# Two model blocks in one kernel: the second block's projection chunks over four PSUM banks, four small transfers on another queue, the last branch's gated product left in its bank

## The reference

```python
# first block
h = rms_norm(x, mix_norm_g)
ys, gate_logit = _token_mixers(h, w_in, ...)       # four kinds of attention, 4 heads of 64 each
branch = einsum('bsnc,ncd->bsnd', ys, w_branch)    # four branches, 256 -> 1024
gates = sigmoid(gate_logit)
x = x + sum(gates * branch, axis=2) @ w_out
x = x + square(relu(rms_norm(x, mlp_norm_g) @ w_up)) @ w_down
x = rms_norm(x, final_norm_g)
# second block
proj = rms_norm_2(x, norm1_g) @ w_in_2             # 1024 -> 2560: q, k, v (512 each), u (1024)
q, k = apply_rope(rms_norm_2(q, ...)), apply_rope(rms_norm_2(k, ...))
attn = moba_attention(q, k, v)                     # 8 heads of 64; with 256 tokens causal softmax attention
conv = conformer_conv(u, ...)                      # GLU, causal depthwise conv of 31 taps, layer norm, silu
x = x + concatenate([attn, conv]) @ w_out_2
x = x + (silu(h @ w_gate_2) * (h @ w_up_2)) @ w_down_2
```

## Time and profile before

| | |
|---|---|
| median of 3 runs | 812.22 us (812.01 to 813.08) |
| the profiled execution's own time | 809.01 us |
| its span | 807.2 us |
| PE busy | 782.7 us, 97% of the span |
| DVE busy | 477.3 us, 59% |
| ACT busy | 408.3 us, 51% |
| POOL busy | 44.2 us, 5% |
| transfers | 136.25 MB, mean 169 GB/s |
| granted TensorE clock | 1.0 in all 40 slices |

### The profile page before, as it was taken

One profiled execution on the slowest core, in us unless ns is written; L12 is line 12 of the kernel. 1 busy time (PEld: TensorE's weight loads), 2 busy tenths in 40 slices (PEclk: granted clock), 3 DMA queues, 4 the chain that ended last, 5 costly groups with the idle time before them and its releaser, 6 DMA issues.

```text
span 807.2 us, 9725 instructions
## 1 busy us (share of the span) xinstructions
PE 782.7 (97%) x3930; PEld 657.4 (81%) x3930; DVE 477.3 (59%) x623; ACT 408.3 (51%) x542; POOL 44.2 (5%) x38
## 2 busy tenths in 40 slices
PE   7999999999999999999999999989999999999998
PEld 5887889878888878888888887767987888888896
DVE  6654364656766877554445448589956654545434
ACT  6565455455656636455444446555556443443341
POOL 1000000000001410000000005011000000000000
PEclk9999999999999999999999999999999999999999
DMA  9842424434445356555655555736123654655341
GB/s 331 319 158 84 151 79 158 149 112 158 156 158 189 124 193 226 198 184 175 208 176 188 180 186 186 283 111 207 56 60 134 224 195 172 207 165 200 104 157 53
DMA packets 68509, 136.25 MB, mean 169 GB/s; under 512 B 2417, under 2 KB 7153, under 8 KB 67825
## 3 DMA queue, kind: packets, MB, share of 16 engines
q1 hardware_dynamic: 68000, 134.44, 49.0%
q10 hardware_dynamic: 464, 1.20, 0.4%
HBM read 134.43 MB, written 1.05 MB: 168 GB/s over the span
## 4 chain that ended last, share of the span: by engine, by line
PE 85%; DVE 9%; ACT 2%; issue 2%; POOL 1%; DMA 1%; SPq 0%; ACTq 0%; DVEq 0%; POOLq 0%
PE b L579 19%; PE b L581 19%; PE b L580 18%; PE SS L579 4%; PE SS L581 4%; PE SS L580 4%; PE TT L548 4%; PE OO L579 2%; PE OO L581 2%; PE OO L580 2%; DVE wlo L1502 2%; DVE ca L1972 1%; PE OO L893 1%; PE SS L662 1%; PE b L719 1%
## 5 line engine op out<-in xcount | busy, mean ns | idle before, releaser
L1502 DVE TENSOR_TENSOR wlo<-raw,whi 128x2048 fp32r<-128x2048 f32 (+2 forms) x123 | 274.2, 2230 | 160.8 <-ACT whi L1061 160.5
L1061 ACT CAST whi<-raw 128x2048 fp32r<-128x2048 f32 (+2 forms) x123 | 227.9, 1854 | 127.5 <-PE b L581 88.0
L579 PE MATMUL b<-whi,Ahi 128*128 128x512 f32 (+2 forms) x568 | 222.2, 391 | 7.4 <-ACT ust L1337 3.4
L581 PE MATMUL b<-whi,Alo 128*128 128x512 f32 (+2 forms) x568 | 215.3, 379 | 0.0
L580 PE MATMUL b<-wlo,Ahi 128*128 128x512 f32 (+2 forms) x568 | 214.7, 378 | 0.0
L579 PEld LDWEIGHTS b<-whi,Ahi 128*128 128x128 f32 x568 | 107.2, 189 | 28.2 <-ACT ust L1337 3.8
L581 PEld LDWEIGHTS b<-whi,Alo 128*128 128x128 f32 x568 | 107.0, 188 | 20.7
L580 PEld LDWEIGHTS b<-wlo,Ahi 128*128 128x128 f32 x568 | 107.4, 189 | 18.3
L579 PE MATMUL b<-whi,Bhi 128*128 128x512 f32 x154 | 60.9, 395 | 0.0
L581 PE MATMUL b<-whi,Blo 128*128 128x512 f32 x154 | 60.0, 390 | 0.0
L580 PE MATMUL b<-wlo,Bhi 128*128 128x512 f32 x154 | 60.0, 390 | 0.0
(11 more groups left out here) (273 smaller groups left out, 1027.0 us busy)
## 6 DMA issues: line engine op xcount, KB each, us to landing
raw<-in_w_in SPq DMA_DIRECT2D x40, 1024.0 KB, 4.9
raw<-in_w_up SPq DMA_DIRECT2D x16, 1024.0 KB, 5.4
raw<-in_w_dn SPq DMA_DIRECT2D x16, 1024.0 KB, 5.0
raw<-in_w_d SPq DMA_DIRECT2D x11, 1024.0 KB, 4.9
raw<-in_w_g SPq DMA_DIRECT2D x10, 1024.0 KB, 4.9
raw<-in_w_u SPq DMA_DIRECT2D x10, 1024.0 KB, 5.0
raw<-in_w_out SPq DMA_DIRECT2D x8, 1024.0 KB, 4.9
raw<-in_w_br SPq DMA_DIRECT2D x4, 1024.0 KB, 4.9
```

Of the source, the lines that this page charges most:

```text
L579: e.matmul(dst, xh, H[:, kc, c0:ce], start=first and kc == krs[0], stop=False)
L581: ins = e.matmul(dst, xl, H[:, kc, c0:ce], start=False, stop=last and kc == krs[-1])
L1061: e.copy(whi[:, s, 0:m], raw[:, r, 0:m]).then_inc(s_hi, 1)
L1502: e.tensor_tensor(wlo[:, s, 0:m], raw[:, r, 0:m], whi[:, s, 0:m].bitcast(F32), ALU.subtract).then_inc(s_lo, 1)
```

## The change

The second block's chunks go to banks (1, 2) and (0, 7) by turns (`P2B`). The four transfers from `odd` to `hp` are issued by SP, between the first two loads of the second block's output weights, and `phases` is gone from ACT; the two constants are copied at step 1 instead of step 9. `rturn` uses banks 5 and 6 by turns. DVE takes the row sums `r0` ahead of the weight split that is due at the same step. One of the 62 taps moves from step 14 to the end of the head loop. The first convolution part stands ahead of head 0's scores. In the first block `sc` and the turn of `pt` take the other bank of 5 and 6 when a `tp` of the same step uses theirs (`other_t`); this changes the bank of two operations, `sc` of head 2 (6 to 5) and of head 3 (5 to 6). For n = 3 `gated` writes gate*branch back into its bank and adds it from there.

```diff
@@ -70,6 +70,8 @@
 BR = [7, 0, 1, 2, 3, 4]
+P2B = [(1, 2), (0, 7)]
 FIRST = [(0, 0), (1, 0), (0, 1), (1, 1)]
@@ -142,7 +144,7 @@
         bg[c].append(("r2", i))
-    for s, n in ((10, 7), (12, 2), (14, 4), (18, 2)):
+    for s, n in ((10, 7), (12, 2), (14, 3), (18, 2)):
         bg[s].append(("cv", n))
@@ -524,6 +526,13 @@
                     e.dma_start(tw[:, q, :], tw_d[:, 2048 * q:2048 * q + 2048]).then_inc(d_tw, 16)
+            if i == unit_of["wo2", 0, 1, 0]:
+                w.wait_ge(s_pad, 1)
+                w.wait_ge(s_ug, 2)
+                for k in range(2):
+                    e.dma_start(hp[64:128, 2 * k, 0:143], odd[0:64, k, 0:143]).then_inc(d_hp, 16)
+                    e.dma_start(hp[0:64, 2 * k + 1, 0:143], odd[64:128, k, 0:143]).then_inc(d_hp, 16)
             load(i)
@@ -594,6 +603,11 @@
+        def other_t(s):
+            bk = next_t()
+            return 11 - bk if bk in [5 + (QP[i][2] // 2) % 2 for name, i in BG1[s] if name == "tp"] else bk
         def next_o():
@@ -622,8 +636,8 @@
-        def sc(h):
-            bk = tbank["sb", h] = next_t()
+        def sc(h, s):
+            bk = tbank["sb", h] = other_t(s)
             w.wait_ge(d_cs1, 32)
@@ -686,13 +700,13 @@
-        def pt(n):
+        def pt(n, s):
             nb = blocks_of(n)
...
                 w.wait_ge(s_e, n + 1)
-            bk = tbank[n] = 5 if nb > 4 else next_t()
+            bk = tbank[n] = 5 if nb > 4 else other_t(s)
             clear(bk)
@@ -750,13 +764,13 @@
                 elif name == "sc":
-                    sc(i)
+                    sc(i, s)
                 elif name == "sp":
...
                 elif name == "t":
-                    pt(i)
+                    pt(i, s)
                 elif name == "pv":
@@ -791,7 +805,7 @@
                             range(2 * (n % 2), 2 * (n % 2) + 2))
-                    gone[bk] = (s_gm, g + 1)
+                    gone[bk] = (s_mix, 2 * hf + t + 1) if n == 3 else (s_gm, g + 1)
                 if hf == 1 and n < 2:
@@ -874,9 +888,9 @@
             w.wait_ge(s_ra, i + 1)
-            clear(5)
-            turn4(bank[5], rope_buf(i)[0]).then_inc(s_rt, 1)
-            gone[5] = (s_q2, i + 1)
+            clear(5 + i % 2)
+            turn4(bank[5 + i % 2], rope_buf(i)[0]).then_inc(s_rt, 1)
+            gone[5 + i % 2] = (s_q2, i + 1)
@@ -936,15 +950,14 @@
                 w.wait_ge(s_xl, X["N2", t, ui] + 1)
-                if ui == 0 and i == 0:
-                    clear(1 + t)
-                elif ui == 0:
-                    w.wait_ge(s_ev, 36 + 2 * (i - 1) + t + 1)
-                product(("p2", i, ui, t), Ahi, Alo, 4 * ui, t, lambda c0, t=t: bank[1 + t], ui == 0, ui == 1)
+                bk = P2B[i % 2][t]
+                if ui == 0:
+                    clear(bk)
+                product(("p2", i, ui, t), Ahi, Alo, 4 * ui, t, lambda c0, bk=bk: bank[bk], ui == 0, ui == 1)
+                gone[bk] = (s_ev, 36 + 2 * i + t + 1)
                 if i == 0 and q == 0:
...
                 stages2(4 * i + q)
-        gone[1], gone[2] = (s_ev, 45), (s_ev, 46)
         n_conv = [0]
@@ -952,10 +965,13 @@
         for k in range(8):
-            az(k)
-            tile_part()
             if k:
+                az(k)
+                tile_part()
                 at(k - 1)
+            else:
+                tile_part()
+                az(k)
             if k < 4:
@@ -1334,7 +1350,7 @@
                 o = V2[:, t, :]
-            e.mul(o, bank[1 + t], r).then_inc(s_ev, 1)
+            e.mul(o, bank[P2B[i % 2][t]], r).then_inc(s_ev, 1)
@@ -1351,7 +1367,7 @@
             w.wait_ge(s_rt, i + 1)
-            src = bank[5].rearrange("p (k q) -> p k q", k=4)
+            src = bank[5 + i % 2].rearrange("p (k q) -> p k q", k=4)
             ts = slice(128 * t, 128 * t + 128)
@@ -1360,14 +1376,6 @@
-        def phases():
-            w.wait_ge(s_pad, 1)
-            w.wait_ge(s_ug, 2)
-            for k in range(2):
-                e.dma_start(hp[64:128, 2 * k, 0:143], odd[0:64, k, 0:143]).then_inc(d_hp, 16)
-                e.dma_start(hp[0:64, 2 * k + 1, 0:143], odd[64:128, k, 0:143]).then_inc(d_hp, 16)
         def am(h):
@@ -1392,11 +1400,6 @@
                     gs(i)
-                elif name == "ug" and i == 1:
-                    phases()
-                    w.wait_ge(d_cs1, 32)
-                    e.copy(identR[:], ident)
-                    e.copy(triR[:], maskF[:, 128:256]).then_inc(s_tri, 1)
                 elif name == "r0":
@@ -1414,6 +1417,10 @@
                 stages2(4 * i + q)
+                if 4 * i + q == 1:
+                    w.wait_ge(d_cs1, 32)
+                    e.copy(identR[:], ident)
+                    e.copy(triR[:], maskF[:, 128:256]).then_inc(s_tri, 1)
                 if 4 * i + q == 7:
@@ -1765,11 +1772,14 @@
                 return
-            e.tensor_tensor(sg, sg, bk, ALU.mult).then_inc(s_gm, 1)
-            if n == 3:
-                w.wait_ge(s_gm, g + 1)
-                w.wait_ge(s_pm, 4 * hf + 2 + t + 1)
-                e.tensor_tensor(mx, mx, sg, ALU.add).then_inc(s_mix, 1)
+            if n < 3:
+                e.tensor_tensor(sg, sg, bk, ALU.mult).then_inc(s_gm, 1)
+                return
+            e.tensor_tensor(bk, sg, bk, ALU.mult).then_inc(s_gm, 1)
+            w.wait_ge(s_gm, g + 1)
+            w.wait_ge(s_pm, 4 * hf + 2 + t + 1)
+            e.tensor_tensor(mx, mx, bk, ALU.add).then_inc(s_mix, 1)
@@ -1990,9 +2000,7 @@
             for name, i in BG2[s]:
-                if name == "r0":
-                    r0(i)
-                elif name == "ra":
+                if name == "ra":
                     ra(i)
@@ -2002,6 +2010,8 @@
                         r1(h)
+                    elif name == "r0":
+                        r0(h)
                 if i == 0 and q == 0:
```

## The result

| | before | changed |
|---|---|---|
| median | 812.12 us (808.88 to 813.08, 4 runs) | 801.16 us (800.8 to 801.46, 4 runs) |
| profiled execution's own time | 809.01 | 800.80 |
| its span | 807.2 | 799.0 |

The ratio is 0.9872 with a 95% interval of 0.9844 to 0.99: 10.96 us shorter, where 8.3 were forecast.

What follows compares the result with a forecast made beforehand. PE's own work plus its waits bound the kernel. First-block sums 1.66 + branch 0.8 + second block 5.60 = 8.06, with refills 8.3 us, taking the median from 812.22 to 803.9; range 802.4 to 807.0.

Steps and rivals of the forecast that it cites:

- the last one of the sum: Carrying the profiled execution's gain over to the median, 3.2 above it: 812.22 - 8.3 = 803.9 us.
- Refill: PE refilling its pipeline after each removed wait: estimated 0.05 to 0.15 us a wait, 0.2 added in all.
- First block's sums: Sums of heads 2 and 3: the other bank removes PE's waits of 0.78 and 0.88, term 1.66 us.
- The branch: Add for n = 3 before the first block's output product: term 0.8 us, between 0.3 loss and 1.2 gain.
- the whole 1.2 can go: Branch: PE's entire 1.2 us wait goes if DVE also keeps its gain at the first half's add.
- the sum by the Trainium skill's rule: Branch: split with two SBUF inputs held until POOL's add ends; term 0.5 us, whole sum 0.3 smaller.
- Second block: Chunks to head 0: evacuation waits go, DVE late next at the first `rturn`; PE gains 5.60 us.
- the last step (0.68): Before head 0's scores: a convolution part fills PE's 0.7 wait for ACT's copy, gaining 0.68 us, to 5.60.
- VectorE in the head loop: Rival: DVE, not PE, sets the head loop's pace; 6.8 us gained, 805.4; chance 0.19.
- A new wait in the chunks in place of the old: Rival: row sums waiting for ACT's squares cost what the transfers' removal gave; 4.5 us gained, 807.7; chance 0.11.
- Nothing: Rival: evacuation waits move to other places of PE and the profile shows 812; chance 0.07.
- slower: Rival: DVE's row sums hold the weight split and PE starves; 814.6 at 13 us late; chance 0.05.

Runs made afterwards that it cites:

- the transfers alone: Kernel before with only the four transfers issued by SP and the two constants copied early, banks staying (1, 2): 809.42 us (10 runs), ratio 0.9964.
- the banks alone: Kernel before with only the second block's chunks using four banks by turns, transfers left on ACT: 808.41 us (5 runs), ratio 0.9963.
- the turn later: Changed kernel with one first-block turn (the one that writes tile 16) a step later, removing PE's wait of 1.76: 797.55 us (4 runs), ratio 0.9824.
- with the taps: Changed kernel with that later turn, plus DVE's seven convolution taps of chunks 3 and 4 put behind the heads: 796.78 us (4 runs), ratio 0.9813.
- the gated product alone: Kernel before with only gate*branch left in its bank and the bank given back after the add: 809.5 us (12 runs), ratio 0.9972.

## Why the prediction was wrong

**The step that failed** is the last one of the sum: "The median of the runs stands 3.2 above that execution and should move by the same". The 3.2 was not a constant that both kernels carry. It was what half clock behind the 2.33 and the 3.38 costs in the usual execution (2.8 in the trace of the kernel before run again; what is left of that trace's gap is a later start), and the change takes away the very waits that it follows. The changed kernel's own half clock, 1.55 behind the wait of 1.76, takes some back: 2.8 - 1.55 = 1.25 net. By the levels it is 1.8, less sharply: that of the usual execution fell by 812.18 - 801.46 = 10.7, that of executions at full clock by 808.81 - 799.86 = 8.95, from two and three executions that scatter.

That the stretches hang on these waits is shown by moving the waits. With the transfers alone the one at the 3.38 is gone and that behind the 2.33 stays; with the banks alone it turns up behind the 3.96. With the second block's edits no trace has one between 500 us and the end of PE's work. With the turn later all eight executions (this edit alone, and with the taps) are at 1.000 or 0.999, where 9 of 12 with the wait were at 0.998. A single trace without a stretch would show little, since the kernel before has such executions too; the count of executions does.

**The sizes** of the three terms account for the other half: 9.56 by starts where 8.3 were added up, 1.26 more. 1.25 + 1.26 and the 0.21 of an earlier start make 2.7, the miss. With either of the two put right alone the forecast would be about 802.6, inside the range: it took both to leave it.
- Refill: "an estimate of 0.05 to 0.15" a wait, 0.2 in all, rests on no row that the prediction names, and is too small. At the earlier trace rows's 2.33 the last matmul ahead starts at 503.43 and the next at 506.14. Undisturbed they start 0.23 apart, so 2.48 is lost, since a matmul of 0.39 overlaps the next by 0.16 and the idle counts from its end. The one behind needs 0.34 instead of 0.23 to the next start. Together 2.59, which is 0.26 more than the 2.33 shown. That is the loss at one wait; the sums' waits lost 0.2 each beyond the idle. PE in order of time, kernel before, the rows on both sides of that one:

```profile
503.43 0.39 PE L581 MATMUL b<-whi,Alo 128*128 128x512 f32 x1
...
506.48 0.40 PE L580 MATMUL b<-wlo,Ahi 128*128 128x512 f32 x1
```

- First block's sums: 2.10 for 1.66, both waits gone as said, the rest refill.
- The branch: 1.26 for 0.8. The add is free of POOL, and the split is held to the end of POOL's adds, as the Trainium skill's rule says: 1.0 less 0.4. But POOL's adds themselves begin 1.37 earlier than in the earlier trace rows (281.17), 0.61 more than the 0.76 by which PE stands earlier there; they are released by DVE's products, and DVE's add at the first half was 1.0 shorter too, with the split behind it 0.4 longer. So DVE kept what it gained there. This is the case named as "the whole 1.2 can go"; the sum by the Trainium skill's rule left that out and was too small.
- Second block: the mechanism held. Chunk 1 was 2.63 for 2.33. DVE is late next, at the first `rturn`: 1.69 for 1.47, since PE arrives earlier by the refills. PE is then 4.90 earlier for 4.51, 5.31 for 4.92, 6.20 for 5.60 at head 0, where the last step (0.68) measured 0.89 and was kept.

**The rivals.** VectorE in the head loop: no, the 0.89 of head 0 reaches the end. A new wait in the chunks in place of the old: no such wait here; the banks alone have one, of 3.96. Nothing, and slower: no.

**Open.** What decides whether a given execution runs at half clock behind such a wait: the same kernel does both. The wait of 1.76 was followed by half clock in 4 of the 5 traces that have both first-block edits, and in 1 of the 7 that have one or none of them (the transfers alone); whether the edits brought it on, no run says. Nor is it known why the gated product alone shifts the stretches.

## What to carry to other kernels

Before a sum is made against one profiled execution, ask whether it is the usual one: its own time (809.01) stood below the lowest of the runs shown (812.01), and that gap was itself a thing to explain, since a change may remove it. A TensorE wait can be worth more than its idle: here 0.2 to 0.26 for the refill and, at the waits of 1.76, 2.33 and 3.38, up to 1.6 more in the executions that ran at half clock behind it. And two edits that each only move a wait can remove it together: look for what is late next behind each alone.

## What the runs showed of the hardware

TensorE's granted clock fell to 0.50 (1.2 GHz) at waits of 1.76 and 1.77, 2.33, 2.34, 3.38 and 3.96, in some executions and not in others, between stretches in which PE was busy. It stayed there for 3.4 us each time, and for 6.8 at the 3.38 in two of three traces; at the 3.38 it fell while PE still stood. At 1.68 to 1.70 before `rturn` it never fell in the seven traces that have such a wait. The digits of the 20 us slices hide it (9 in the changed kernel, one 8 in the kernel before run again): windows of 2 us, or the time of one repeated matmul (0.39 and 0.63), show it.

A 128x512 fp32 product that DVE wrote back into the PSUM bank that it read took 0.68 us, as much as into SBUF, and an add with one input in PSUM took 0.69 beside POOL's adds, where two SBUF inputs took 1.69.
